# Mid-tile attention steps, out projections in rounds, and norm chains for pairs of tiles in a three-layer network

## The reference

```
# layer 0 (retention) and 1 (differential attention)
u = rms_norm(x, w) @ w_in                       # q, k, v, gate, memory q
o_main = silu(g) * rms_norm(retention(q, k, v))                     # layer 0
lam = exp(sum(lq1 * lk1)) - exp(sum(lq2 * lk2)) + lambda_init       # layer 1
a = softmax(q0 k0 + bias) - lam * softmax(q1 k1 + bias)             # layer 1
o_main = rms_norm(a @ v, subln)                                     # layer 1
x = x + concatenate([o_main, o_mem]) @ w_out    # 1024 -> 1024
x = x + (silu(gate) * val) @ w_down             # gate, val = rms_norm(x) @ w_gate_up
# layer 2
z, xbc, dt, q, k, v, f = split(rms_norm(x) @ w_in)
y_ssd = rms_norm(ssd(silu(conv(xbc)), dt) * silu(z))     # 16 heads, 2 groups
q, k = rms_norm(heads(q)), rms_norm(heads(k))            # 16 heads of 64
y_fox = softmax(q k + cum - cum, causal) @ v
x = x + concatenate([y_ssd, y_fox]) @ w_out              # 2048 -> 1024
x = x + conv_gated_mlp(rms_norm(x))
```

## Time and profile before

| | |
|---|---|
| time, median of 3 runs | 1100.18 us (1098.59 to 1103.19) |
| the profiled execution | 1097.26 us, span 1095.5 us, mean TensorE clock 0.995 |
| PE busy | 1052.4 us (96%), 8666 matmuls |
| VectorE busy | 760.9 us (69%) |
| ScalarE busy | 586.6 us (54%) |
| GpSimd busy | 178.8 us (16%) |

### The profile page before, as it was taken

The page is one execution under the profiler, slowest core; times in us unless marked ns, Lnnn a source line. Parts: engine busy times, 40 slices in busy tenths (PEclk is TensorE's granted clock), DMA queues, the critical chain, the costliest instruction groups (busy, mean ns, idle before and its releaser), DMA issues.

```text
span 1095.5 us, 23936 instructions
## 1 busy us (share of the span) xinstructions
PE 1052.4 (96%) x8666; PEld 1013.2 (92%) x8666; DVE 760.9 (69%) x1323; ACT 586.6 (54%) x1047; POOL 178.8 (16%) x186
## 2 busy tenths in 40 slices
PE   5999999999999998999999999989899999999998
PEld 5989999999999877899999999988788999999998
DVE  6876686666555887866666459857877679988843
ACT  6654564444544645654445446655555566666532
POOL 4100121111110000411111110000212023444300
PEclk9999999999999999999999999999999999999999
DMA  7533455555565321555555654433232455555563
GB/s 279 179 134 106 144 175 185 180 180 179 178 194 165 124 88 53 189 178 186 184 180 176 194 184 141 172 115 136 78 116 71 133 196 179 175 188 176 167 208 103
DMA packets 51480, 174.45 MB, mean 159 GB/s; under 512 B 5840, under 2 KB 7120, under 8 KB 51280
## 3 DMA queue, kind: packets, MB, share of 16 engines
q1 hardware_dynamic: 51408, 173.46, 47.5%
HBM read 172.39 MB, written 1.05 MB: 158 GB/s over the span
## 4 chain that ended last, share of the span: by engine, by line
PE 80%; DVE 14%; ACT 3%; issue 2%; POOL 1%; DMA 1%; SPq 0%; DVEq 0%; POOLq 0%; ACTq 0%
PE bank L678 23%; PE bank L679 23%; PE bank L680 23%; DVE ring_lo L1447 4%; DVE xw_lo L1453 1%; ACT tmp L1212 1%; PE bank L663 1%; PE bank L665 1%; PE bank L664 1%; PE bank L788 1%; ACT tmp L1269 1%; PE bank L879 1%; PE bank L977 1%; DVE root_parts L1651 1%; PE bank L899 1%
## 5 line engine op out<-in xcount | busy, mean ns | idle before, releaser
L678 PE MATMUL bank<-xw_hi,ring_hi 128*128 128x256 f32 x1576 | 452.0, 287 | 2.6 <-ACT lam L1347 1.1
L679 PE MATMUL bank<-xw_lo,ring_hi 128*128 128x256 f32 x1576 | 446.0, 283 | 0.0
L680 PE MATMUL bank<-xw_hi,ring_lo 128*128 128x256 f32 x1576 | 445.8, 283 | 0.0
L1447 DVE TENSOR_TENSOR ring_lo<-ring_raw,ring_hi 128x1024 fp32r<-128x1024 f32 (+2 forms) x338 | 402.3, 1194 | 57.9 <-ACT ring_hi L1031 52.2
L1031 ACT ACTIVATE ring_hi<-ring_raw 128x1024 fp32r<-128x1024 f32 (+2 forms) x338 | 341.2, 1012 | 90.5 <-PE bank L680 84.5
L678 PEld LDWEIGHTS bank<-xw_hi,ring_hi 128*128 128x128 f32 x1576 | 302.3, 192 | 8.3 <-issue 3.7
L679 PEld LDWEIGHTS bank<-xw_lo,ring_hi 128*128 128x128 f32 x1576 | 302.4, 192 | 0.2
L680 PEld LDWEIGHTS bank<-xw_hi,ring_lo 128*128 128x128 f32 x1576 | 302.3, 192 | 0.0
L678 PE MATMUL bank<-act_hi,ring_hi 128*128 128x256 f32 x736 | 211.6, 288 | 11.0 <-DVE ring_lo L1853 7.5
L679 PE MATMUL bank<-act_lo,ring_hi 128*128 128x256 f32 x736 | 209.3, 284 | 0.0
L680 PE MATMUL bank<-act_hi,ring_lo 128*128 128x256 f32 x736 | 209.2, 284 | 0.0
(11 more groups left out here) (193 smaller groups left out, 1180.6 us busy)
## 6 DMA issues: line engine op xcount, KB each, us to landing
ring_raw<-w_up SPq DMA_DIRECT2D x132, 512.0 KB, 3.2
ring_raw<-w_in SPq DMA_DIRECT2D x85, 512.0 KB, 3.2
ring_raw<-w_down SPq DMA_DIRECT2D x48, 512.0 KB, 3.5
ring_raw<-w_down SPq DMA_DIRECT2D x24, 384.0 KB, 3.8
ring_raw<-w_ob SPq DMA_DIRECT2D x10, 512.0 KB, 3.8
ring_raw<-w_oa SPq DMA_DIRECT2D x16, 256.0 KB, 2.6
ring_raw<-w_oa SPq DMA_DIRECT2D x8, 512.0 KB, 3.6
ring_raw<-w_kv SPq DMA_DIRECT2D x7, 512.0 KB, 6.9
```

Of the source, the lines that this page charges most:

```text
L678: mm(bank[b][:, 0:T], w_hi, tile(hi, t), start=kk == 0, stop=False)
L679: mm(bank[b][:, 0:T], w_hi, tile(lo, t), start=False, stop=False)
L680: last = mm(bank[b][:, 0:T], w_lo, tile(hi, t), start=False, stop=end)
L1447: V.tensor_tensor(ring_lo[:, a:b], ring_raw[:, a:b], ring_hi[:, a:b].bitcast(f32), SUB).then_inc(lo_done, 1)
```

## The change

1. oa0/ob0 and oa1/ob1 become oc0/oc1, 8 full tiles each in rounds: a tile holds 2 K steps for 4 outputs, in the order of ROUNDS (pair of inputs, half of the outputs). The eight outputs lie in four banks, two in each, and are all finished in the last two tiles. x is then added in four pieces of 512 columns. Layer 2 keeps oa2 and ob2.
2. Each phase starts to count its banks anew.
3. Steps named in HALFWAY (spreads in layer 1, pair_spread and ssd_out in layer 2) are issued by PE in the middle of the following tile instead of between the tiles. VectorE takes ssd_skip, norm_out and pair_out last among its EARLY steps in layers 1 and 2.
4. The q and k norms of layer 2 become four chains of 256 columns, each for a pair of q tiles and a pair of k tiles; fox slots are one later. The weights of the SSD have a second pair of buffers. ssd_decay picks with one matmul of 384 columns in place of two.
5. At the start, the first mean square stands after tile 2 of kv in place of tile 1, its last two squares are summed by PE (L713 has three matmuls then) in place of GpSimd, and x's splits and squares are spread over the first tiles.
6. lam's exp moves from the head of in1 to slot 1 of layer 0. The silus of g's first two thirds move from slot 19 to 18, their products to 18 and 19.

```diff
-          ("in0", 20, [8], 20), ("oa0", 8, [6], 8), ("ob0", 2, [8], 2), ("up0", 44, [8], 4), ("down0", 24, [8, 8, 6], 12),
-          ("in1", 20, [8], 20), ("oa1", 8, [4], 8), ("ob1", 4, [8], 4), ("up1", 44, [8], 4), ("down1", 24, [8, 8, 6], 12),
+          ("in0", 20, [8], 20), ("oc0", 8, [8], 8), ("up0", 44, [8], 4), ("down0", 24, [8, 8, 6], 12),
+          ("in1", 20, [8], 20), ("oc1", 8, [8], 8), ("up1", 44, [8], 4), ("down1", 24, [8, 8, 6], 12),
...
+ROUNDS = [(0, 0), (1, 0), (0, 1), (1, 1), (2, 0), (2, 1), (3, 0), (3, 1)]
...
+        return (self.out(i if type(i) is int else 0, c) - self.out0) % self.banks
...
+    def freed_out(self, n):
+
+        b = self.bank_of[n]
+        return max((m + 1 for m in range(n) if self.bank_of[m] == b), default=0)
...
-        plan[layer][slot + 2].insert(0, ("spread", tile))
+        plan[layer][slot + 2].insert(0, ("spread_soon" if soon or slot >= 20 and layer == 1 else "spread", tile))
...
+    at(0, 1, "lam", 0)
...
+    for half_, slot, kind in ((0, 18, "gated"), (1, 19, "gated_soon"), (2, 20, "gated")):
+        at(0, 20 if half_ == 2 else 18, "gate_silu", half_)
+        at(0, slot, kind, half_)
     for half_, slot in ((0, 19), (1, 19), (2, 20)):
-        at(0, slot, "gate_silu", half_)
-    for half_, slot in ((0, 19), (1, 19), (2, 20)):
-        at(0, slot, "gated", half_)
...
-    norm(1, 23, 10 + 64, True)
+    norm(1, 22, 10 + 64, True)
...
-    for k, slot in ((6, 11), (7, 11), (0, 19), (1, 19), (2, 23), (3, 23), (4, 26), (5, 26)):
+    for k, slot in ((6, 11), (7, 11), (0, 19), (1, 19), (2, 23), (3, 23), (4, 25), (5, 25)):
...
-        norm(2, a + 2, 20 + 2 * j)
-        norm(2, a + 4, 28 + 2 * j)
+        at(2, a + 2, "pair_squares", j, 0)
+        at(2, a + 4, "pair_squares", j, 1)
+        at(2, a + 5, "pair_norm", j)
+        for which in range(2):
+            plan[2][a + 6 + which].insert(0, ("pair_spread", j, which))
+            plan[2][a + 7 + which].insert(0, ("pair_out", j, which))
         for n in range(2):
-            p, slot = 2 * j + n, a + 7 + 3 * n
+            p, slot = 2 * j + n, a + 8 + 3 * n
             at(2, slot, "fox_scores", p)
...
-    for g, slot in ((0, 28), (1, 40)):
+    for g, slot in ((0, 29), (1, 36)):
...
+        X_SPLITS = {1: (3,), 2: (4, 5), 3: (6,), 4: (7,)}
+        X_SQUARES = {1: (0, 1), 2: (2, 3), 3: (4, 5), 4: (6, 7)}
...
+                        if halfway and k == 2:
+                            halfway(c)
...
+                    if halfway and k == ph.blocks[part] // 2:
+                        halfway(c)
...
+            def project_rounds(layer, then, halfway):
+
+                ph = PH[f"oc{layer}"]
+                for c, (pair, half) in enumerate(ROUNDS):
...
+                            pe.wait_ge(sm_m, so_far["scores"])
+                    for j in range(4):
+                        if j == 2:
+                            halfway(c)
+                        m = 4 * half + j
+                        b = m // 2
+                        if pair == 0 and half == 0 and j % 2 == 0:
+                            pe.wait_ge(out_ready, ph.freed_out(ph.out0 + b))
+                        o = bank[b][:, (m % 2) * T:(m % 2) * T + T]
+                        for k in range(2):
+                            t = ph.inputs[2 * pair + k]
+                            if m == 0:
+                                pe.wait_ge(mix_lo, number["mix", (layer, t)] + 1)
+                            a = slot * DM + (2 * j + k) * P
+                            w_hi, w_lo = ring_hi[:, a:a + P], ring_lo[:, a:a + P]
+                            mm(o, w_hi, tile(act_hi, t), start=pair == 0 and k == 0 and m % 2 == 0, stop=False)
+                            mm(o, w_hi, tile(act_lo, t), start=False, stop=False)
+                            last = mm(o, w_lo, tile(act_hi, t), start=False, stop=pair == 3 and k == 1 and m % 2 == 1)
+                        if pair == 3 and j == 1:
+                            last.then_inc(ob_done, 1)
+                    last.then_inc(tile_done, 1)
+                    then(c)
+
             def mean_square(q):
...
+                if q == 0:
+                    mm(bank[7][:, 0:T], cmat("ones1024"), sqsum, start=True, stop=False)
+                    pe.wait_ge(sq_done, KT)
+                    for r in (KT - 2, KT - 1):
+                        last = mm(bank[7][:, 0:T], cmat("ones1024"), two(sq, r % 2), start=False, stop=r == KT - 1)
+                    last.then_inc(ms_done, 1)
+                    return
...
-                    if c == (1 if name == "kv" else 0) and q is not None:
+                    if c == (2 if name == "kv" else 0) and q is not None:
...
+            def pair_norm(layer, j):
...
+                    pe.wait_ge(act_small, 7)
+                for d in range(4):
+                    last = mm(bank[4][32 * d:32 * d + 32, 0:T], cmat("means64", 32),
+                              normed(d // 2)[:, d % 2 * T:d % 2 * T + T], start=True, stop=True)
+                last.then_inc(np_ms, 1)
...
+            def pair_spread(layer, j, which):
+
+                if which == 0:
+                    pe.wait_ge(np_nt, 5 * pair_no(j) + 5)
+                else:
+                    pe.wait_ge(np_out, outs_of[pair_no(j)] - 1)
+                for m in range(2):
+                    d = 2 * which + m
+                    last = mm(bank[4][:, m * T:(m + 1) * T], spread_r[:, d * P:(d + 1) * P], root_parts[:, :],
                               start=True, stop=True)
                 last.then_inc(np_bc, 1)
...
+            HALFWAY = ((), ("spread",), ("pair_spread", "ssd_out"))
...
-                        if kind in DO:
+                        if kind in DO and kind not in HALFWAY[layer]:
                             DO[kind](layer, *key)
                 return then
+
+            def amid(layer, slot0):
+
+                def halfway(c):
+                    if slot0 + c:
+                        for kind, *key in PLAN[layer][slot0 + c - 1]:
+                            if kind in HALFWAY[layer]:
+                                DO[kind](layer, *key)
...
-                if layer == 1:
-                    pe.wait_ge(lam_in, 1)
-                    mm(bank[5][:, 0:2], con[0:64, CCOL["ones1024"]:CCOL["ones1024"] + P], lam[0:64, 0:2],
-                       start=True, stop=True).then_inc(lam_ps, 1)
-                    pe.wait_ge(lam_e, 1)
                 n_in = PH[f"in{layer}"].n
-                run(f"in{layer}", xw_hi, xw_lo, stream_ready(q), q, follow(layer, 0))
-                run(f"oa{layer}", act_hi, act_lo, mixed_ready(layer), None, follow(layer, n_in))
-                project_group(layer)
+                run(f"in{layer}", xw_hi, xw_lo, stream_ready(q), q, follow(layer, 0), amid(layer, 0))
+                if layer < 2:
+                    project_rounds(layer, follow(layer, n_in), amid(layer, n_in))
+                else:
+                    run("oa2", act_hi, act_lo, mixed_ready(2), None, follow(2, n_in), amid(2, n_in))
...
+                for c in range(ph.n):
+                    early(ph, 0, c)
+                    if c >= 6:
+                        for p in (2 * c - 12, 2 * c - 11):
+                            if p % 2 == 0:
+                                dve.wait_ge(ob_done, 2 * layer + p // 2 + 1)
+                            else:
+                                dve.wait_ge(tile_done, ph.tile(0, c)[1] + 1)
+                            two_out = x[:, 2 * p * T:(2 * p + 2) * T]
+                            V.tensor_tensor(two_out, two_out, bank[p][:, :], ADD).then_inc(out_ready, 1)
+                            if p:
+                                stream_lo(q, 2 * p - 2, x)
+                                stream_lo(q, 2 * p - 1, x)
+                    if c == 7:
+                        stream_lo(q, 6, x)
+                        stream_lo(q, 7, x)
+                    middle(ph, 0, c)
+                    split_lo(ph, 0, c)
+                    late(ph, 0, c)
 
...
+                    if layer and kinds is EARLY:
+                        planned = sorted(planned, key=lambda step: step[0] in ("ssd_skip", "norm_out", "pair_out"))
...
-            EARLY = {"norm_out", "softmax", "ssd_weights", "ssd_skip", "fox_probs"}
-            MIDDLE = {"group_out"}
+            EARLY = {"norm_out", "pair_out", "softmax", "ssd_weights", "ssd_skip", "fox_probs"}
+            MIDDLE = {"group_out", "gated_soon"}
```

269 lines of the change are left out of this document (177 added, 92 removed).

## The result

The changed kernel takes 1090.47 us (median of 5 runs, 1089.3 to 1091.83) against 1100.18 of the kernel before: a ratio of 0.9908, 95% interval 0.9887 to 0.9929. It is faster by 9.7 us, 0.9%. The forecast was 21.2 us faster, 1079, and the range ended at 1089: the direction was right and the size was not.

The account below looks back on a forecast made before the run. TensorE (PE), busy 96% of the span, was taken as the bound; gains of -28.6 us and costs of +7.4 gave -21.2, a median of 1079 us against 1100.18, with a range of 1070 to 1089.

Parts of the forecast that it names:

- Layer 2, -12.0 foretold: Layer 2's terms: halfway steps -7.7, third L977 wait -1.5, its clock fall -0.9, pair norms -1.9 us.
- I leave 1.0: Layer 2's halfway steps: of 8.7 us of waits, 1.0 was to remain, giving -7.7 us.
- Pair norms -1.9: Layer 2: four 256-column chains cost PE 4.9 us where eight of 128 columns cost 6.8; range 0 to -3.4.
- Up projections, +3.1 foretold: Start of both up projections: x arrives in one burst, PE stalls 2 us per layer; +3.1 us (0 to +5).
- Layer 1 in and out, -6.5 foretold: Layer 1's terms: halfway steps and a clock fall -5.2, out projection -5.1, bank wait +2.1, clock behind it +1.7 us.
- the bank wait: Layer 1's first out tile: PE waits 2.5 us for the in-projection's last evacuation; +2.1, plus +1.7 us for the clock.
- Leave 0.5: Layer 1's in-projection: of 4.0 us of spread waits 0.5 was to remain, giving -3.5 us.
- I leave 0.8: Layer 1's out projection: doubled tiles cover 5.6 us and more of waits, 0.8 remains; -5.1 us (-3 to -5.9).
- Layer 0's in and out, -4.0 foretold: Start of layer 0's out projection: earlier silus close the act_lo wait, 2.3, and the clock's fall, 1.7 us; 0 to -4.3.
- lam, -1.1 foretold: Head of layer 1's in-projection: PE's 1.1 us wait for lam's exp goes once the exp moves to layer 0.
- the start, -1.2 foretold: Kernel start: PE waits 2.7 us for GpSimd's adds; one add counted as saved, -1.2 us (0 to -2.4).
- Rival A: Gains half realised, chance 0.18: VectorE's queue moves with PE, waits reappear half a tile on; -12 us, 1088.

Follow-up runs that it names:

- single chains: The changed kernel with eight norm chains of 128 columns in layer 2 in place of four of 256: layer 2's in and oa 228.9 us against 228.6.
- the repaired kernel: The changed kernel plus bank 1 start, inputs 2 and 3 first, last ring_lo behind x's splits, norm_out first (layer 1), pair_norm first: 1076.83 us, ratio 0.9779.

## Why the prediction was wrong

By its own sum, against the profiled executions (-21.2 foretold, -6.6 measured; the medians lie 9.7 apart):

- **Layer 2, -12.0 foretold, -7.9 measured.** The mechanism was right: halfway steps are worth 13.7 us there against the same kernel without them. The failed step is "I leave 1.0" of the waits, with "Pair norms -1.9". The pair chain stood behind a softmax in the queues of ScalarE and VectorE and kept 4.3 us of waits and a fall of the clock; single chains came out equal. PE's work for a pair was as assumed (0.57 us for the sums where 0.55 was taken, 0.24 to 0.33 for each of two spreads where 0.34 was), so "Pair norms -1.9" failed by the waits and not by the work. With the pair chain first in its slot, in and oa took 223.8 us, 12.8 less than before: the foretold -12.0 was to be had by the order alone (the repaired kernel, with one fall of the clock there, is 11.2 below). The wait behind z's silu was 1.6 us where 1.9 was foretold, and the clock did not fall behind it.
- **Up projections, +3.1 foretold, +8.6 measured.** The sum had only the stall. Measured without a fall it is 130.9 us in both layers: 2.1 and 3.2 over before, 5.3 together, so the stall was itself sized 2.2 too small: a ring_lo of 1.76 us stands ahead of the adds and was left out of the sum. The rest, 3.3 us, is three periods at the lower clock, for which there was no term. GpSimd beside VectorE makes most of the stall.
- **Layer 1 in and out, -6.5 foretold, -2.0 measured.** The first 16 in tiles gained 4.4 us, and the bank wait was 2.6 where 2.5 was foretold (worth 1.6 when it was closed), though the clock did not fall behind it. Two steps failed. "Leave 0.5" of the spreads: behind the 18th tile the next norm's squares and the last norm's spread were waited for 1.9 and 1.1 us. The first of these waits hung on norm_out behind a softmax, and before the change a wait of 1.1 us for a spread (at 417.19 us) stood right ahead of the same squares and hid it. And "I leave 0.8" of the out projection: it took the doubled tiles as cover and missed that the rounds need inputs 2 and 3 early, which cost 2.0 us and a fall; with these two split first the out projection took 30.05 us, 4.9 less than before where 5.1 was foretold. The prediction's own sign for this, no wait over 0.5 us in layer 1's oc tiles, failed by that one wait.
- **Layer 0's in and out, -4.0 foretold, -4.3 measured, mostly for the wrong reason.** The mixes moved from 119.03 to 117.55 us, 1.5 earlier and not the 2.87 of a slot, since the silus' table load stands behind the last norm's roots, for which ScalarE waits until 113.52 us for PE's sums; the silus passed only the rounding of one ring tile, which now stands between them and the mixes. With the silus early and the rounds off, PE still waited for act_lo, 1.1 us in one run, where in and out took 0.8 us less than before, and 1.7 in the other, where the clock fell and nothing was gained. So 0 to 0.8 of the 4.3 us are the silus' and 3.4 the rounds', whose first tile needs two inputs in place of six: the number came out by luck. The new bank numbers, put at nothing in layer 0, go with 0.6 us more in its in-projection (80.13 against 79.54 in the run with the old ones). Of the rule on table loads in the Trainium skill, "ScalarE: Activation LUTs", section "What ACT_TABLE_LOAD costs": the trace after, ScalarE,

```profile
113.92 0.31 ACT L1281 ACTIVATE roots_b<-roots_b 128x128 f32<-128x128 f32 x1
114.25 1.28 ACT L1329 ACT_TABLE_LOAD   x1
115.55 1.15 ACT L1329 ACTIVATE u<-u 128x512 f32<-128x512 f32 x2
...
117.55 1.32 ACT L1358 ACTIVATE act_hi<-u 128x256 fp32r<-128x256 f32 x4
```

shows the load 0.02 us behind the instruction ahead of it and the silu 0.02 us behind the load's end. By the Trainium skill's rule a drain of 1.38 us would come on top of the load; the trace does not agree.

- **lam, -1.1 foretold, -1.6 measured; the start, -1.2 foretold, -0.6 measured**, which is less than the start varies between runs that don't touch it. The +0.5 for breaking tiles has no stretch of its own; behind a spread in the middle of a tile, the first two projection matmuls are 0.17 us apart in place of 0.12 (403.88 and 404.05 us in the changed kernel), 0.05 as assumed. Layer 2's down projection grew by 1.2, not foretold; it goes with the pair chains, by a way that stays open.

Rival A, "the queue moves along with PE and the wait reappears", is nearest to what happened, at 1088. It would have 9 us of the gains stay away, and in layer 2 and layer 1 8.6 did; the other 5.5 us, in the up projections, it didn't have. Its ground, a full VectorE, isn't what the runs show: steps moved ahead in the same queues closed the waits. The cover was taken as 12 matmuls for each step, while a step's date depends on what stands ahead of it in two queues, and PE, earlier with each wait closed, gets to it sooner.

## What to carry to other kernels

Closing a wait moves an in-order engine ahead, towards the next date of the chain that fed it. So a gain is not the sum of the waits closed: follow each chain to its end and ask what it stands behind in each queue. When several outputs finish together, count what the late burst does to VectorE with GpSimd beside it, and price the clock's fall behind every new stall. A chain that is short but late is mended by its place in the order: five repairs, four of order and one of a bank, took the changed kernel from 1090.5 to 1076.8 us, and two squares summed by PE in place of GpSimd in each of two layers took it to 1074.3.

## What the runs showed of the hardware

- GpSimd's additions (two SBUF inputs) slow VectorE's instructions that have two inputs in SBUF: a split of 128x256 takes 0.81 us beside them and 0.47 without, a ring_lo of 128x1024 1.76 and 1.22. The Trainium skill, "GPSIMD Engine Reference", section "1. Specifications", says that the two share their SBUF interfaces and contend where VectorE's instruction has two SBUF inputs; these rows agree.
- A fall of the clock to 1.2 GHz lasts 3.4 us in these profiles. It costs 0.8 to 1.6 us where PE is the bound (layer 0's up projection took 131.71 and 132.43 us with one fall against 130.93, layer 1's out projection 34.27 against 32.71, layer 2's in-projection 181.11 against 179.57) and nothing where PE waits behind it anyway: layer 1's in-projection took 88.17 us without one and 88.15 with one at 408.9 to 412.4. Where it falls differs between kernels at the same wait: behind the bank's wait near 424 us it fell in nine of the thirteen profiles that have this wait, and not in four, the changed kernel's among them.
